# The norm stage by tile, the next half's blocks loaded during the last pair, and a reordered first chunk, in a hybrid conv, HGRN2 and delta-rule layer

## The chip, the cores and the metric

The kernel runs on one core of one Trainium2 chip. The metric is the device time of one execution in microseconds; the median of three runs stands for the kernel. TensorE, VectorE (DVE), ScalarE (ACT), GpSimd (POOL) and SyncE (SP, which only issues DMAs here) run in parallel, each in the order of its own program, and meet at semaphores.

## The reference

One layer on 2048 tokens of 1024 channels. A projection of the normalised input feeds three mixers (a short convolution, HGRN2, a gated delta rule in chunks), whose results are merged by sigmoid gates:

```python
h = rmsnorm(x, norm_w)
proj = einsum('bsd,dc->bsc', h, w_in)        # split into 15 parts
gates = sigmoid(g_all + b_gate)
y_a = (a_b * causal_dwconv(a_c * a_x, conv_a) * silu(a_z)) @ w_out_a
y_b = (head_rmsnorm(hgrn2_chunked(q, k, v, log_f), w) * silu(b_z)) @ w_out_b
y_c = (head_rmsnorm(gated_delta_chunked(q, k, v, log_a, beta), w) * silu(c_z)) @ w_out_c
merged = gates[0] * y_a + gates[1] * y_b + gates[2] * y_c
out = rmsnorm(x + merged @ w_o, final_norm_w)
```

The delta rule solves (I + M) s = rhs for each chunk, M being strictly lower triangular; the kernel's chunks are 128 tokens.

## The kernel before

Five parts run one after the other, each in its own function, with a barrier of all engines between them: `constants`, `norm_and_transpose`, `project`, `recur` and `merge`.

`norm_and_transpose` goes over the 16 tiles t of 128 tokens. ScalarE's `statistics(t)` squares and sums a row of x and makes the reciprocal root; VectorE's `normalise(t)` scales x into `xn`; TensorE's `turn(t)` transposes it in eight 128x128 pieces into PSUM; VectorE's `weigh(t)` multiplies by the norm's weights and writes it. Tiles 0 to 7 (the first half of the tokens) stay on the chip in `hraw`, as four blocks B11, B12, B21, B22 of 512 channels by 512 tokens; tiles 8 to 15 go to DRAM (`h_scratch`) through `ht`, a ring of four tiles. Beside it TensorE forms 16 small columns (beta and the decay) with `sums_of(g)`, once for each group of four tiles, `columns_of(g)` turns them, and `table(g)` copies them. The projection multiplies in Strassen's way with seven products P1 to P7: for each, a combination of the blocks is split into a high part (`h_high`, fp32r, by ScalarE) and a low part (`h_low`, the rest). GpSimd makes the lows of P1, P2 and P5, VectorE those of P3, P7, P6 and P4 and the four block sums (`block_sum`). Dictionaries `after` put these steps behind certain tiles. SP loads x into `xin` (three tiles), and after the last store the first weights.

`project` goes over 80 pairs of column tiles, 40 on each half of the tokens. Pair p has seven products of 12 matmuls (128x512): TensorE's order is P1(p), P4(p-1), P2(p), P3(p-1), P6(p), P5(p), P7(p), and both of pair 39's late ones follow at once. ScalarE copies X to m1, u2 and u3 between products and splits the next weights (`high_part`), GpSimd makes their lows (`low_part`), VectorE their sums and takes the results into `craw`. SP loads weights of pair p+2 and stores results from a `ring` of four slots. After pair 39 the blocks of the second half are needed: `load_tokens` waits for its last product and loads four 1 MB blocks into `h_low`, `token_sums` (DVE) makes the four combinations in `craw`, `ring` and `work`, `token_highs` (ACT) and `token_lows` (POOL and DVE) split them, each in one piece in the engines' programs.

`recur` goes over 16 chunks w. For each the inverse of I + M is built: the 16x16 blocks on the diagonal by substitution on VectorE (`blocks_out` takes ak through DRAM into `X`, `substitute`, `inverses_back` through DRAM into `TT` and `R`), then three levels of doubling on TensorE (`level_w`, `level_z`), then r, e, o and the state. Work of chunk w+1 and the scores of HGRN2 are interleaved. Ahead of chunk 0 come the columns, its key norms, decays (`log_decays`, `betas`, `weighted_decays` on GpSimd), products and its inverse's blocks; `fill_masks` on GpSimd makes the masks. `T`, `R` and `b_g` in the trace are TT, R and the PSUM banks G.

## Time and profile before

| what | value |
|---|---|
| median of 3 runs (2977.01 to 2982.47) | 2977.89 us |
| profiled execution, its own time | 2978.44 us |
| its span, from the first instruction to the last | 2976.7 us |
| TensorE busy in matmuls, share of the span | 2761.7 us, 93% |
| VectorE, ScalarE, GpSimd busy | 1868.9, 1236.1, 1545.4 us |
| mean granted TensorE clock, share of full speed | 0.968 |

A timeline row reads: start and length in us, engine, line of the kernel, operation, out<-in by the program's names (buffer numbers left out), shapes, count of instructions merged, and in brackets how long the engine was idle before it and what ended that. Where rows are merged, the length is that of the whole stretch. Ends of matmuls are modelled, so that consecutive ones seem to overlap; their starts are exact. PEclk is the clock granted to TensorE as a share of 2.4 GHz, so 0.50 is 1.2 GHz.

### The profile page before, as it was taken

How to read it: one execution, taken by the hardware profiler on the slowest of the kernel's cores; microseconds unless marked ns; L12 is line 12 of the kernel's file. 1: busy time of each engine (PE TensorE's matmuls, PEld its weight loads, DVE VectorE, ACT ScalarE, POOL GpSimd, SP SyncE). 2: the span in 40 equal slices, each digit the busy share in tenths (PEclk: the TensorE clock that was granted, in tenths of full speed). 3: DMA queues.
4: the chain of work that ended last, by engine and by line, in shares of the span. 5: the costliest groups of instructions: out<-in, count | busy, mean ns of one | idle time of the engine just before them, and what ended most of it. 6: DMA issues, size and time to landing. Idle time of an engine off the chain costs nothing. (4 is left out here: it accounts for less than half of the span.)

```text
span 2976.7 us, 39010 instructions
## 1 busy us (share of the span) xinstructions
PE 2761.7 (93%) x13943; PEld 2293.6 (77%) x13943; DVE 1868.9 (63%) x2886; ACT 1236.1 (42%) x2144; POOL 1545.4 (52%) x1161
## 2 busy tenths in 40 slices
PE   5799999999987999999999779999999869999999
PEld 2488888888865888888888568888888757787877
DVE  6568778772228778877723278888888643444453
ACT  5244434444443434444444345555555433122221
POOL 1355555455437455555554466676666375353531
PEclk7899999999998999999999989999999989999999
DMA  4332333334441433333333455445555266555552
GB/s 137 97 111 83 119 92 107 107 99 114 113 151 47 120 92 107 104 102 116 92 107 105 123 140 126 126 124 145 147 148 133 54 192 207 153 168 164 165 172 82
DMA packets 535879, 363.92 MB, mean 122 GB/s; under 512 B 65430, under 2 KB 469000, under 8 KB 535688
## 3 DMA queue, kind: packets, MB, share of 16 engines
q1 hardware_dynamic: 535688, 361.43, 42.6%
q8 instruction: 113, 1.85, 0.3%
q14 instruction: 78, 0.64, 0.1%
HBM read 249.17 MB, written 112.20 MB: 121 GB/s over the span
## 5 line engine op out<-in xcount | busy, mean ns | idle before, releaser
L715 POOL TENSOR_TENSOR w_low<-w_raw,w_high 128x512 fp32r<-128x512 f32 x480 | 682.9, 1428 | 623.2 <-ACT w_high L793 623.1
L747 PE MATMUL p_x<-h_high,w_high 128*128 128x512 f32 x1280 | 501.8, 392 | 33.0 <-POOL h_low L722 17.8
L747 PE MATMUL p_x<-h_high,w_low 128*128 128x512 f32 x1280 | 500.4, 391 | 0.0
L747 PE MATMUL p_x<-h_low,w_high 128*128 128x512 f32 x1280 | 500.4, 391 | 0.0
L793 ACT ACTIVATE w_high<-w_raw 128x512 fp32r<-128x512 f32 x480 | 297.2, 626 | 256.3 <-PE p_z L747 142.5
L747 PEld LDWEIGHTS p_x<-h_high,w_high 128*128 128x128 f32 x1280 | 241.9, 189 | 86.0 <-issue 18.2
L2185 POOL TENSOR_TENSOR m_wo_low<-m_wo_raw,m_wo_high 128x512 fp32r<-128x512 f32 x128 | 172.5, 1352 | 252.7 <-ACT m_wo_high L2275 252.7
L747 PEld LDWEIGHTS p_x<-h_low,w_high 128*128 128x128 f32 x1280 | 241.8, 189 | 50.6
L747 PEld LDWEIGHTS p_x<-h_high,w_low 128*128 128x128 f32 x1280 | 242.0, 189 | 50.0
L2226 PE MATMUL b_o<-m_yh,m_wo_high 128*128 128x512 f32 x512 | 208.1, 406 | 55.5 <-POOL m_wo_low L2185 31.9
L747 PE MATMUL p_z<-h_high,w_high 128*128 128x512 f32 x640 | 249.0, 389 | 0.0
L747 PE MATMUL p_z<-h_high,w_low 128*128 128x512 f32 x640 | 249.0, 389 | 0.0
L747 PE MATMUL p_z<-h_low,w_high 128*128 128x512 f32 x640 | 249.0, 389 | 0.0
L1009 DVE TENSOR_TENSOR c_raw<-p_z,u 128x512 f32<-128x512 f32 x72 | 49.8, 691 | 250.8 <-PE p_x L747 181.3
L2226 PE MATMUL b_o<-m_yh,m_wo_low 128*128 128x512 f32 x512 | 206.1, 403 | 0.0
L2226 PE MATMUL b_o<-m_yl,m_wo_high 128*128 128x512 f32 x512 | 205.5, 401 | 0.0
L2275 ACT ACTIVATE m_wo_high<-m_wo_raw 128x512 fp32r<-128x512 f32 x128 | 80.7, 631 | 282.8 <-PE b_o L2226 234.3
L2319 DVE TENSOR_TENSOR m_tmp<-b_o,m_gt 128x512 f32<-128x512 f32 x96 | 66.4, 692 | 205.2 <-PE b_o L2226 144.9
L715 POOL TENSOR_TENSOR w_low<-w_s,w_high 128x512 fp32r<-128x512 f32 x80 | 115.0, 1438 | 96.1 <-ACT w_high L793 95.5
L2226 PEld LDWEIGHTS b_o<-m_yh,m_wo_high 128*128 128x128 f32 x512 | 100.3, 196 | 82.0 <-POOL m_wo_low L2185 35.5
L1369 POOL TENSOR_TENSOR dx<-hin 128x256 f32<-128x256 f32 x112 | 76.9, 686 | 158.7 <-ACT hx L1720 157.1
L1025 DVE SCALAR_TENSOR_TENSOR ring<-c_raw,cols,ring 128x512 f32<-128x512 f32 x128 | 142.5, 1113 | 4.6
(282 smaller groups left out, 6131.8 us busy)
## 6 DMA issues: line engine op xcount, KB each, us to landing
w_raw<-in_w_in_dram SPq DMA_DIRECT2D x160, 512.0 KB, 5.2
branch_scratch<-ring SPq DMA_DIRECT2D x176, 256.0 KB, 5.2
gate_scratch<-ring SPq DMA_DIRECT2D x96, 256.0 KB, 6.0
m_gt<-gate_scratch SPq DMA_DIRECT2D x96, 256.0 KB, 3.8
hin<-branch_scratch SPq DMA_DIRECT2D x16, 1280.0 KB, 11.0
zin<-branch_scratch SPq DMA_DIRECT2D x16, 1024.0 KB, 6.4
m_yl<-y_scratch SPq DMA_DIRECT2D x16, 1024.0 KB, 10.3
m_wo_raw<-in_w_out_c_dram SPq DMA_DIRECT2D x64, 256.0 KB, 2.9
```

The costliest lines, as they stand in the source:

```text
L715: nc.gpsimd.tensor_tensor(wl[:, j, :, :], place(p, j), wh[:, j, :, :].bitcast(F32), ALU.subtract).then_inc(low, 1)
L747: x = nc.tensor.matmul(to[:], w[:, j, k, :], h[:, j, k, :], start=(opens and k == 0 and a == 0), stop=(k == HK - 1 and a == 2), skip_group ...
L793: fn(wh[:, j, :, :], place(p, j), ACT.Copy).then_inc(high, 1)
L1009: tt(of_unit(p, 1, 1), Z[p % 2][:], u3[:], ALU.add).then_inc(c22, 1)
L1025: link(stt(out, src, w, out, ALU.mult, ALU.add))
L1369: tt(free_ap(dx[:, l % 2, :], 0, halves), left, mid, ALU.subtract)
L2185: tt(wl[:, u % SLOTS, :, :], wraw[:, u % SLOTS, :, :], raw(wh[:, u % SLOTS, :, :]), ALU.subtract).then_inc(w_low, 1)
L2226: x = nc.tensor.matmul(bank, w[:, u % SLOTS, k, :], y[:, 4 * i + k, :], start=(i < 3 and k == 0 and a == 0), stop=(i != 2 and k == 3 and a ...
L2275: fn(wh[:, u % SLOTS, :, :], wraw[:, u % SLOTS, :, :], ACT.Copy).then_inc(w_high, 1)
L2319: tt(to, bank, gt[:, b, :], ALU.mult).then_inc(gated, 1)
```

## The change

**Norm stage.** The sums are made tile by tile (`sums_of(t)`, eight products of 128 columns instead of eight of 512 for each group). All seven low parts and the block sums are VectorE's; GpSimd has no work in the stage. `normalise(t)` is ScalarE's from tile 8 on. `xin` has four tiles, `xn` three, `ht` two; SP loads the first weights ahead of the last five stores.

TensorE at the start of the stage, before (with seven more rows of this kind to its end):

```order
L356 MATMUL ps_h<-ident,xn 128x128 x40
L367 MATMUL ps_s<-hraw,wsm 16x512 x8
L356 MATMUL ps_h<-ident,xn 128x128 x24
L375 MATMUL ps_s<-ident,small 128x16 x4
L356 MATMUL ps_h<-ident,xn 128x128 x8
```

and after it:

```order
L366 MATMUL ps_h<-ident,xn 128x128 x16
L378 MATMUL ps_s<-hraw,wsm 16x128 x8
L366 MATMUL ps_h<-ident,xn 128x128 x8
L378 MATMUL ps_s<-hraw,wsm 16x128 x8
L366 MATMUL ps_h<-ident,xn 128x128 x8
```

The transposes of tile t+1 stand between the sums of two tiles; at the end of the stage the sums of one tile are left in place of those of four.

**Change of halves.** `load_tokens`, `token_sums`, `token_highs` and `token_lows` are gone. Each block goes by `load_block` to a place that is free early: b11 to `work`, b12 to the low part of P2, b22 to that of P6, b21 to that of P5, and b21 and b22 once more, to those of P4 and P3. P7's sum is made in two halves in a new tile `t3`, so the places free up earlier. SP issues these loads between its stores within pair 39, ScalarE and VectorE have their steps between those of pairs 39 and 40; GpSimd makes P3's low only.

VectorE around the change of halves, before; `c_raw<-p_z,u` are the takes of pair 39, `w_s<-w_raw` begins the weight sums of pair 41:

```order
L1009 TENSOR_TENSOR c_raw<-p_z,u 128x512
L1014 TENSOR_TENSOR c_raw<-p_z,u 128x512
L956 TENSOR_TENSOR c_raw<-h_low 128x2048
L959 TENSOR_TENSOR c_raw<-h_low,c_raw 128x2048
L962 TENSOR_TENSOR ring<-h_low,c_raw 128x2048
L963 TENSOR_TENSOR work<-h_low 128x2048
L967 TENSOR_TENSOR h_low<-c_raw,h_high 128x2048
L967 TENSOR_TENSOR h_low<-work,h_high 128x2048
L967 TENSOR_TENSOR h_low<-ring,h_high 128x2048
L971 MEMSET c_raw 128x4x3
L979 TENSOR_TENSOR w_s<-w_raw 128x512
```

and after it, from the last sum that is made within pair 39:

```order
L1010 TENSOR_TENSOR work<-h_low,work 128x2048
L1077 TENSOR_TENSOR c_raw<-p_z,u 128x512
L1016 TENSOR_TENSOR t<-h_low 128x1024
L1023 TENSOR_TENSOR c_raw<-h_low,work 128x2x1024
L1041 TENSOR_TENSOR h_low<-t,h_high 128x1024
L1016 TENSOR_TENSOR t<-h_low 128x1024
L1082 TENSOR_TENSOR c_raw<-p_z,u 128x512
L1041 TENSOR_TENSOR h_low<-h_low,h_high 128x2048
L1041 TENSOR_TENSOR h_low<-c_raw,h_high 128x2048
L1041 TENSOR_TENSOR h_low<-work,h_high 128x2048
L1030 TENSOR_TENSOR ring<-h_low,c_raw 128x2048
L1041 TENSOR_TENSOR h_low<-t,h_high 128x1024
```

P5's sum (L1010) now stands ahead of the take of c22, and P1's low three rows before it; P7's pieces are on both sides of the take of c12.

SP in the same place has, in place of one group of four loads behind all stores, these rows within pair 39 (load, stores, loads by turns):

```order
L693 DMA work<-h_scratch 128x4x512
L712 DMA gate_scratch<-ring 128x512 x3
L693 DMA h_low<-h_scratch 128x4x512 x2
L712 DMA gate_scratch<-ring 128x512
L693 DMA h_low<-h_scratch 128x4x512
L683 DMA w_raw<-in_w_in_dram 128x8x128 x2
L712 DMA gate_scratch<-ring 128x512 x2
```

Before, the weights stood ahead of all of pair 38's stores, and the blocks behind all of pair 39's.

**First chunk.** The squares of chunk 0 are ScalarE's and its `betas` VectorE's; GpSimd goes from `log_decays(0)` to the masks and `weighted_decays(0)`, and `pairs` and the squares of chunk 1 come behind. VectorE splits the log decays before it clears the states. The mask `later` is gone (it is ones minus `causal`). Chunk 0's diagonal blocks are inverted in the bank G[1] instead of M[0], which frees M[0] for other products in that time, and these are moved ahead of its inverse: v, k, hv, products_ks, scores 0 to 2 of chunk 0 and the decays and products of chunk 1.

TensorE in front of chunk 0's first inverse product (`b_g<-T,ak`), before:

```order
L1473 MATMUL b_m<-qkn 128x256 x4
L1446 MATMUL b_m<-sq,ones 128x512 x2
L1484 MATMUL b_m<-ident,zin 128x128 x8
L1494 MATMUL b_m<-S,qkn 128x256 x4
L1543 MATMUL b_g<-T,ak 128x128 x8
L1500 MATMUL b_m<-ident,qkn 128x128 x4
```

and after it (`b_h<-kql` are the scores; behind it level_z follows at once):

```order
L1577 MATMUL b_m<-S,qkn 128x256 x4
L1583 MATMUL b_m<-ident,qkn 128x128 x4
L1589 MATMUL b_m<-ident,hin 128x128 x4
L1609 MATMUL b_h<-kql 128x128 x4
L1533 MATMUL b_m<-la_t,later_r 128x512 x4
L1609 MATMUL b_h<-kql 128x128 x4
L1533 MATMUL b_m<-la_t,ones_r 128x512 x4
L1556 MATMUL b_m<-qkn 128x256 x4
L1609 MATMUL b_h<-kql 128x128 x4
L1626 MATMUL b_g<-T,ak 128x128 x8
```

Eight groups of matmuls that stood behind the first inverse product now stand ahead of it. The core of the diff:

```diff
@@ norm_and_transpose @@
-    XIN, XN, SETS = 3, 2, 3
+    XIN, XN, HT, SETS = 4, 3, 2, 3
...
-                for t in range(1, T):
+                for t in range(2, T):
                     load(t)
-                    if t - 3 >= first:
-                        store(t - 3)
-                for t in range(T - 3, T):
-                    store(t)
+                    if t - XIN - 1 >= first:
+                        store(t - XIN - 1)
                 for u, col in enumerate(front["first"]):
                     sp.dma_start(front["raw0"][:, u, :, :], io["w_in"][0, :, col:col + P].rearrange("(k p) c -> p k c", p=P)).then_inc(w0_in, 16)
-                for i in range(per):
-                    sp.wait_ge(h_out[i], 16 * ((T - first) // per))
+                for t in range(T - XIN - 1, T):
+                    store(t)
...
+                    if t >= first:
+                        normalise(t)
...
-                after = {8: [lambda: block_sum(P5)], 9: [lambda: block_sum(P7), lambda: table(0), lambda: low(P3)], 10: [lambda: block_sum(P6)],
-                         11: [lambda: low(P7)], 12: [lambda: block_sum(P4), lambda: table(1)], 13: [lambda: low(P6)], 14: [lambda: low(P4)], 15: [lambda: table(2)]}
+                after = {5: [lambda: low(P1)], 6: [lambda: low(P2)], 7: [lambda: table(0)], 8: [lambda: block_sum(P5)],
+                         9: [lambda: block_sum(P7), lambda: low(P3)], 10: [lambda: block_sum(P6)], 11: [lambda: block_sum(P4), lambda: low(P5)],
+                         12: [lambda: table(1), lambda: low(P7)], 13: [lambda: low(P6)], 14: [lambda: low(P4)], 15: [lambda: table(2)]}
...
-                def sums_of(g):
-                    pe.wait_ge(weighed, 2 * per * (g + 1))
-                    if g >= 2:
+                def sums_of(t):
+                    g, u = t // per, t % per
+                    pe.wait_ge(weighed, 2 * t + 2)
+                    if g >= 2 and u == 0:
                         pe.wait_ge(tabbed, g - 1)
                     for k in range(K):
-                        h = hraw[:, 2 * (k // HK) + g, k % HK, :] if g < 2 else ht[:, :, k, :]
-                        x = nc.tensor.matmul(ps_s[g % 2][0:2 * V, :], wsm[:, k, :], h, start=(k == 0), stop=(k == K - 1))
+                        h = hraw[:, 2 * (k // HK) + g, k % HK, u * P:(u + 1) * P] if t < first else ht[:, t % HT, k, :]
+                        x = nc.tensor.matmul(ps_s[g % 2][0:2 * V, u * P:(u + 1) * P], wsm[:, k, :], h, start=(k == 0), stop=(k == K - 1))
...
@@ project @@
+        b_place = {"b11": work[:], "b12": lows_of(P2), "b22": lows_of(P6), "b21": lows_of(P5), "b21_again": lows_of(P4),
+                   "b22_again": lows_of(P3)}
+        b_free = {"b12": P2, "b22": P6, "b21": P5, "b21_again": P4, "b22_again": P3}
+        b_block = {"b11": (0, 0), "b12": (0, 1), "b22": (1, 1), "b21": (1, 0), "b21_again": (1, 0), "b22_again": (1, 1)}
...
+        b_order = (P1, P5, (P7, 0), P6, P2, (P7, 1), P4, P3)
+        sum_order = (P5, (P7, 0), P6, (P7, 1), P4)
+        pool_lows, dve_lows = (P3,), (P1, (P7, 0), P2, P6, P5, (P7, 1), P4)
...
+                    if p in last_of and p + 1 < N:
+                        sb, late = pairs[p][0] + 1, [x for x in results if x[0] == p]
+                        load_block(sb, "b11")
+                        for x in own[:-1]:
+                            store(x)
+                        load_block(sb, "b12")
+                        load_block(sb, "b22")
+                        store(own[-1])
+                        load_block(sb, "b21")
+                        load_weights(p + 2)
+                        for x in late[:2]:
+                            store(x)
+                        load_block(sb, "b21_again")
+                        store(late[2])
+                        load_block(sb, "b22_again")
+                        store(late[3])
+                        continue
...
+                    half_ends, sb = p in last_of and more, pairs[p][0] + 1
+                    if half_ends:
+                        token_low(sb, P1)
                     if q is not None:
                         finish_mid(q)
                         take_c12(q)
                     if more:
                         fourth_sum(p + 1)
+                    if half_ends:
+                        token_sum(sb, P5)
...
+                            token_sum(sb, (P7, 0))
+                            token_sum(sb, P6)
+                            token_low(sb, (P7, 0))
+                            token_sum(sb, (P7, 1))
                         take_c12(p)
                         finish_late(p)
                         finish_last(p)
-                        if more:
-                            token_sums(pairs[p][0] + 1)
+                        if half_ends:
+                            token_low(sb, P2)
+                            token_low(sb, P6)
+                            token_low(sb, P5)
+                            token_sum(sb, P4)
+                            token_low(sb, (P7, 1))
...
+                    if p in last_of and more:
+                        token_high(pairs[p][0] + 1, P1)
+                    if p - 1 in last_of:
+                        token_high(pairs[p][0], P4)
...
+                        token_high(pairs[p][0], P3)
                     if q is not None:
                         finish_late(q)
                     if more:
                         high_part(p + 1, P5)
+                    if p in last_of and more:
+                        token_high(pairs[p][0] + 1, P5)
...
+                            token_high(pairs[p][0] + 1, (P7, 0))
                         if p in x_by_act:
                             from_x(p)
                         finish_mid(p)
+                        if more:
+                            token_high(pairs[p][0] + 1, P6)
+                            token_high(pairs[p][0] + 1, P2)
+                            token_high(pairs[p][0] + 1, (P7, 1))
...
@@ recur @@
-        XP = free_ap(M[0][0:V * NB, 0, :], 0, [[SUB, SUB], [1, SUB]])
+        XP = lambda v: free_ap((M[0] if v > 0 else G[1])[0:V * NB, 0, :], 0, [[SUB, SUB], [1, SUB]])
...
-                squares(0)
-                pool.wait_ge(split, 3)
+                pool.wait_ge(split, 2)
                 log_decays(0)
-                betas(0)
                 fill_masks(pool, more_masks, masks_set, masks_cut)
+                weighted_decays(0)
+                differences(0, 0)
+                squares(1)
                 tt(pairs[:], keep["ident"][:], more_masks["upper"][:, 0, :], ALU.add).then_inc(pairs_set, 1)
-                weighted_decays(0)
-                squares(1)
+                differences(0, 1)
                 log_decays(1)
                 betas(1)
-                differences(0, 0)
                 pool.wait_ge(cols, 2)
...
+                turn_v(0)
+                norms(1)
+                pe.wait_ge(zeroed, 4)
                 pe.wait_ge(col_exp, 1)
-                norms(1)
+                products_ks(0)
+                turn_k(0)
+                turn_hv(0)
+                scores(0, 0)
+                decays_between(1)
+                scores(0, 1)
+                decays_from_start(1)
+                products_kq(1)
+                scores(0, 2)
...
+                copy_v(0)
+                level_exp(0, 0)
                 blocks_in(0)
+                key_norms(1)
+                copy_k(0)
+                copy_hv(0)
+                level_exp(0, 1)
+                from_start_h(0)
                 inverses_out(0)
-                key_norms(1)
-                level_exp(0, 0)
+                decays_between(1)
+                decays_from_start(1)
+                level_exp(0, 2)
...
+                pair_kq(0)
                 unit_diagonal(0)
                 substitute(0, range(SUB - 2, 0, -1))
+                dve.wait_ge(cols, 2)
+                residual(0)
+                keys(1)
                 dve.wait_ge(masks_cut, 2 * LEVELS + 2)
                 dve.wait_ge(pairs_set, 1)
-                dve.wait_ge(cols, 2)
+                level_kq(0, 1)
+                pair_scores(0)
+                an_keys(1)
+                an_queries(1)
...
```

## Rows read from the trace of the kernel before

**Rows 1.** Windows: us, busy and count of PE, PEld, DVE, ACT, POOL, PEclk, DMA share, GB/s

```profile
24.00:28.00 4.00, 3.62 (x11) 1.85 (x11) 1.57 (x3) 2.39 (x2) 0.40 (x1) 0.50 0.72 252
28.00:32.00 4.00, 4.00 (x10) 0.93 (x9) 2.85 (x1) 3.90 (x8) 4.00 (x1) 0.92 0.01 4
...
1150.00:1200.00 50.00, 50.00 (x223) 41.40 (x222) 46.34 (x47) 20.86 (x35) 26.91 (x19) 1.00 0.31 88
```

**Rows 2.** Timeline of TensorE, norm stage to the first product

```profile
24.43 1.97 PE L356 MATMUL ps_h<-ident,xn 128*128 128x128 f32 x8 [0.38 <-DVE xn L395]
...
34.45 1.10 PE L356 MATMUL ps_h<-ident,xn 128*128 128x128 f32 x8
...
71.26 9.60 PE L367 MATMUL ps_s<-ht,wsm 128*16 128x512 f32 x16 [1.43 <-DVE ht L407]
...
114.18 0.79 PE L747 MATMUL p_x<-h_high,w_high 128*128 128x512 f32 x1 [7.50 <-POOL w_low L715]
```

**Rows 3.** Timeline of TensorE, change of halves

```profile
878.65 0.39 PE L747 MATMUL p_z<-h_low,w_high 128*128 128x512 f32 x1
896.83 0.76 PE L747 MATMUL p_x<-h_high,w_high 128*128 128x512 f32 x1 [17.79 <-POOL h_low L722]
...
912.12 0.77 PE L747 MATMUL p_y<-h_high,w_high 128*128 128x512 f32 x1 [9.83 <-POOL h_low L722]
...
930.88 0.50 PE L747 MATMUL p_x<-h_high,w_high 128*128 128x512 f32 x1 [3.02 <-ACT u L922]
...
948.09 0.79 PE L747 MATMUL p_x<-h_high,w_high 128*128 128x512 f32 x1 [3.30 <-ACT u L912]
```

**Rows 4.** Timeline of TensorE, first chunk of the recurrence

```profile
1734.83 2.05 PE L1543 MATMUL b_g<-T,ak 128*128 128x128 f32 x16 [0.48 <-DMA T<-inverse_scratch]
...
1755.01 1.95 PE L1566 MATMUL b_g<-r,R 128*128 128x128 f32 x16
```

**Rows 5.** Timeline of VectorE, norm stage

```profile
29.15 3.53 DVE L395 TENSOR_SCALAR xn<-xin,stat 128x1024 f32<-128x1024 f32 x1 [3.58 <-ACT stat L317]
...
41.54 1.29 DVE L407 TENSOR_TENSOR hraw<-ps_h,cols 128x512 f32<-128x512 f32 x2 [0.17 <-PE ps_h L356]
...
51.91 2.29 DVE L428 TENSOR_TENSOR hraw<-hraw 128x2048 f32<-128x2048 f32 x1 [4.42 <-PE ps_s L367]
```

**Rows 6.** Timeline of ScalarE, norm stage

```profile
12.98 1.06 ACT L313 ACTIVATE xn<-xin 128x1024 f32<-128x1024 f32 x1 [2.42 <-DMA xin<-in_x_dram]
...
14.82 1.06 ACT L313 ACTIVATE xn<-xin 128x1024 f32<-128x1024 f32 x1
...
105.62 0.59 ACT L330 ACTIVATE small<-ps_s 16x512 f32<-16x512 f32 x1 [16.46 <-PE ps_s L367]
```

**Rows 7.** Timeline of ScalarE, change of halves

```profile
872.66 0.60 ACT L922 ACTIVATE u<-p_x 128x512 f32<-128x512 f32 x1 [2.09 <-PE p_x L747]
...
886.71 1.91 ACT L802 ACTIVATE h_high<-h_low 128x2048 fp32r<-128x2048 f32 x1 [4.88 <-DMA h_low<-h_scratch]
```

**Rows 8.** DMA issues in 8 to 112: count, KB each, median us to landing

```profile
h_scratch<-ht SPq DMA_DIRECT2D x8, 512.0 KB, 3.4
```

**Rows 9.** Timeline of SP, change of halves

```profile
880.92 2.48 SPq L666 DMA_DIRECT2D h_low<-h_scratch  x4
```

**Rows 10.** Timeline of VectorE, change of halves

```profile
898.88 6.53 DVE L962 TENSOR_TENSOR ring<-h_low,c_raw 128x2048 f32<-128x2048 f32 x1
```

**Rows 11.** Timeline of GpSimd, first chunk of the recurrence

```profile
1694.72 3.80 POOL L1348 TENSOR_TENSOR la_t<-causal,la_parts 128x1024 fp32r<-128x1024 f32 x2
...
1700.79 0.84 POOL L124 MEMSET upper<- 128x896 f32 x1
...
1709.82 2.34 POOL L1358 TENSOR_TENSOR dec<-dec,db 128x1024 f32<-128x1024 f32 x1
```

**Rows 12.** Timeline of VectorE, first chunk of the recurrence

```profile
1690.88 0.29 DVE L1999 TENSOR_TENSOR la_parts<-ab,la_parts 128x128 fp32r<-128x128 f32 x1
...
1726.70 0.17 DVE L1891 TENSOR_TENSOR b_m<-b_m,part 64x14 f32<-64x14 f32 x1
```

332 lines of the change are left out of this document (187 added, 145 removed).

## The prediction

> **What bounds the kernel now.** I went first by the timeline of TensorE, looking for stretches in which it does not start its next matmul at once. In a settled stretch of the projection it starts one every 50 / 223 = 0.224 us [rows 1], and nothing here is faster than that. Three places differ, and the change touches these three: the normalisation stage in front of the first product at 114.18 [rows 2], the change of halves after the matmul at 878.65 [rows 3], and the first chunk of the recurrence, whose first inverse product starts at 1734.83 [rows 4]. So I cost each place by itself, as the time at which TensorE gets back to its regular work, and add the three. The projection between them and the merge behind them are left as they are; what is gained in front of a place moves it as a whole. The profiled execution took 2978.44 us (span 2976.7); the sum is made against that and 0.5 us taken off for the median 2977.89.
>
> **Part 1, the normalisation.** What is there now: a group of sums is one burst of 9.60 us on TensorE [rows 2], and VectorE waits for it (4.42 us ahead of the block sum at 51.91) [rows 5]; a normalisation that meets GpSimd's low parts takes 3.53 us [rows 5] where the shape costs about 0.75. VectorE finishes the weighing of tile 7 at 41.54 + 1.29 = 42.8 [rows 5]; the small copy of the last group starts at 105.62 [rows 6], and from there to the first product are 114.18 - 105.62 = 8.6 us of short steps that the change keeps.
>
> The first eight tiles after it: ScalarE's statistics take 14.82 - 12.98 = 1.84 us a tile [rows 6], but high(P1) still waits for tile 3, and VectorE now carries low(P1) and low(P2), 2 x 2.29 [rows 5], where GpSimd's collisions used to cost about as much. TensorE adds a quarter of a group (9.60 / 4 = 2.4) to 1.10 or 1.97 of transposes per tile [rows 2]. I walk this to 44.6, 1.8 later than now.
>
> The last eight: VectorE has 8 weighings of 1.29, 4 block sums and 5 lows of 2.29 [rows 5]: 10.3 + 20.6 = 30.9 us. ScalarE, which takes over the eight normalisations (about 1.06 each, as its square of the same 128x1024) [rows 6], has 8 x (1.84 + 1.06) + 5 x 1.91 [rows 6, 7] + 2 x 0.59 = 33.9, of which the first tile lies ahead of 44.6: 31.0. Two engines that hand work to each other with nearly equal sums do not run without waits, and a weighing also waits for the store two tiles before (3.4 us to land [rows 8], behind a load, and from tile 13 on behind the first weights too). I add 4: the weighing of tile 15 ends at 44.6 + 30.9 + 4 = 79.5. Then one tile's sums (2.4), the copy and the 8.6 to the first product: 90.5, and 2.5 more for matmuls at the lower clock: 93. **Gain 114.2 - 93 = 21.** Ends: no waits and full clock give 27; the rival below gives 10.
>
> TensorE's order is now eight transposes of a tile, then eight products of 128 columns for the sums of the tile before; it works in short bursts. In the trace it was granted 0.50 (1.2 GHz) in 24 to 28, after transposes with waits between them, and 0.92 in 28 to 32, once sums kept it busy without a gap [rows 1]. The Trainium skill (TensorE: Matmul & The Clock Gate, section A second HAM failure mode: psum-queue depth-cycling) says that small idles between groups of matmuls make the clock go down and up, and that the stream loses by it. The trace agrees in part, by the fall to 0.50; by that rule the first product would be later by the 9 to 12 us of rival 1.
>
> **Part 2, the change of halves.** Now: the last matmul starts at 878.65; the next are at 896.83, 912.12, 930.88 and, after 60 more, 948.09 [rows 3]. Between 878.65 and 948.09 stand 132 matmuls (11 products of 12), 29.6 us at 0.224: 69.4 - 29.6 = **39.8 us are lost**. The load is issued at 880.92 [rows 9], the first 1 MB is used at 886.71 [rows 7], 5.8 us later, and sums and lows follow one another, one of them stretched to 6.53 by GpSimd [rows 10] against 2.29 alone [rows 5].
>
> After: the first block goes to `work` some 26 us earlier, the others as the last products of the low parts that they overwrite end (a product is 12 x 0.224 = 2.7 us, pair 39 has its seven up to 878.9). P1's high and low are made inside the pair, so product P1 of pair 40 starts right behind P3 of pair 39. What it costs there: ScalarE's u3 copy (872.66 now, [rows 7]) stands behind high(P5), which waits for b12, issued after the stores of pair 38 that it follows in SP's queue. b12 lands about 868.8, sum and high add 2.3 (more beside GpSimd) and 1.9: u3 at 874.4 instead of 872.7. **-1.7.** The rest is VectorE's chain from u3 on: take_c22, half of P7's sum (1.2), P6's sum (2.3), low of the half, the other half's sum, then low P2, low P6, low P5 (2.2 each), sum P4, low of the other half (the rows stand with the change). Walked from u3, the lows end so: P2 done at 885.1, P6 887.3, P5 889.5, P7 892.8, P4 897. TensorE: P1 880.5, P2 waits until 885.2 (2.0 lost), P6, P5 without wait, P7 waits for u2, which ScalarE copies only after high(P4), which needs sum P4 at 891.7: 895.9 (2.5 lost). P3 is cut by GpSimd after 898.3 and needed at 906.8: covered, with 2 us to spare if it takes 6.5. At the place of 948.09 the wait hangs on VectorE's convolution of pair 40, which starts when weights 42 land; they are issued about 30 us earlier, the wait stays, 2.7. Sum: 1.7 + 2.0 + 2.5 + 2.7 = 8.9 lost in place of 39.8. **Gain 30.5** (I round down for the seams). Ends: 34 with no collision on the ports, 20 with rival 2.
>
> The stores of pair 39 and the weights 41 move behind block loads on SP's queue; they are late by 3 to 6 us, and their readers (ring slots, early_sums(41) at 893) come later still. Nothing.
>
> **Part 3, the first chunk.** GpSimd's weighting of dec starts at 1709.82 [rows 11], after squares, la_t (3.80), db, the masks (from 1700.79) and pairs. Now it is la_t (after la_parts, which VectorE makes first: 1689.5 instead of 1691.2 [rows 12]), masks with 1709.82 - 1700.79 = 9.0, then dec: 1689.5 + 3.8 + 9.0 = 1702.3, **7.5 earlier**. The masks stay in front of it; dec itself is ready at about 1700. From there the chain through DRAM (store, X, substitution until 1726.70 [rows 12], store, T) is as long as before, so T is there at 1734.83 - 7.5 = 1727.3.
>
> But TensorE now has scores(0,2) ahead of its first inverse product, and that needs level_kq(0,2), which stands on VectorE behind residual, keys(1), an_keys(1) and an_queries(1), all behind the substitution (ends 1719.4). Walked: 11 us at full clock, 15 at half. So the inverse product starts between 1730.5 and 1734.5; I take 1732.5. In return it is not interleaved: before, 20.2 us pass from there to the product with r at 1755.01 [rows 4]; 20 matmuls of 128 columns at 0.11 (1.10 for eight, in [rows 2] a little over it), 8 of 512 at 0.224 and 4 of 256 at twice a column's cost leave: 2.2 + 1.8 + 1.8 = 5.8. 20.2 - 5.8 = 14.4, so r's product starts at 1746.9: **gain 8**. Behind it nothing moved. Ends: 13.3 (7.5 + 5.8, no gate) and 2.
>
> **Sum.** 21 + 30.5 + 8 = 59.5; 2978.4 - 59.5 - 0.5 = 2918.4, **2918**.
>
> **Rivals.**
> 1. TensorE stays at 1.2 GHz through the second eight tiles: 1.97 + about 3.5 (a quarter group without the faster half) = 5.5 a tile, 44 us instead of 34.9, and the tail 2 longer: gain 10, time **2929**. For it: 0.50 in [rows 1]. Against: at that pace it would have no gaps, and the same rows show the clock rising when it has none. 0.13.
> 2. Port collisions at the change of halves: five 2048-wide operations of VectorE behind u3, each longer by 2 (the row shows up to 4.2 more [rows 10]). Gain 20, **2929**. Against: GpSimd has no weights to cut between 877 and 887. 0.13.
> 3. The gate in the first chunk eats all of its gain: **2926**. 0.08.
> 4. Slower: the two-deep `ht`. Each tile's weighing waits for a store that SP issues behind a load whose slot waits for ScalarE. If load, store and weighing ran one after the other (4 + 3.4 + 1.3 = 8.7 a tile, 70 us for eight), part 1 would lose 14 instead of gaining 21: 2953. It turns the whole slower only from 59.5 + 35 more, at 8.7 + 3.5 = about 13 us a tile: **2990**. Against it: 3.4 to land is for 512 KB alone, and the loads are four tiles ahead. 0.02.
> 5. The planned order does not start earlier at one of the three places, because a wait that I took as met is not: 2940. 0.03.
>
> **Chances.** Forecast 0.61 (2908 to 2927 by itself). Cases 1 to 3 lie at 2926 to 2929 and two together near 2937; the upper ends of all three gains together give 2904. Range **2903 to 2936**. A measurement of this kernel tells about 0.2%, 6 us, from no change. Faster 0.97, same 0.01, slower 0.02.
>
> **What would show it.** First product of the projection near 93, with sums of 2 to 3.5 us behind every tile's transposes; if it is above 100, look at the granted clock there. At the change of halves no gap over 4 us, product P1 of pair 40 within 3 us of the last one of pair 39, a gap ended by ScalarE's u ahead of P7. T's product near 1732 less what is gained before it (about 51), so near 1681, ended by VectorE's kql and not by the DMA of T; 14 to 15 us from it to r's product. Wrong is the forecast if GpSimd or a DMA ends a wait of over 5 us in one of them.

## The result, and the profile after

| | before | after |
|---|---|---|
| median | 2978.34 us (2977.01 to 2982.47, 4 runs) | 2924.90 us (2924.39 to 2925.99, 4 runs) |
| ratio | | 0.9819, 95% interval 0.9802 to 0.9836 |
| profiled execution, span | 2978.44, 2976.7 us | 2925.99, 2924.3 us |
| mean granted clock | 0.968 | 0.979 |

The kernel is 53.4 us faster; 2918 was forecast, and 59.5 us of gain. I read the three places again as I had read them before: the time at which TensorE gets back to its regular work.

**The normalisation.** Timeline of TensorE (start, us, instruction, then in brackets the idle time ahead of it and what ended it), from the last tile's sums to the first product of the projection:

```profile
77.09 1.92 PE L378 MATMUL ps_s<-ht,wsm 128*16 128x128 f32 x16
79.69 0.42 PE L386 MATMUL ps_s<-ident,small 16*128 16x16 f32 x4 [0.68 <-ACT small L338]
87.61 0.80 PE L788 MATMUL p_x<-h_high,w_high 128*128 128x512 f32 x1 [7.50 <-POOL w_low L758]
```

The first product starts at 87.61 instead of 114.18 [rows 2]: 26.6 gained. The windows of this stage (length, then busy time and count of PE, PEld, DVE, ACT and POOL, the granted clock, DMA share, GB/s) hold the main surprise, the clock:

```profile
24.00:28.00 4.00, 4.00 (x35) 3.15 (x34) 2.51 (x4) 0.53 (x1) 0.00 (x0) 1.00 0.59 221
28.00:32.00 4.00, 3.01 (x26) 2.39 (x27) 0.98 (x2) 3.94 (x6) 0.00 (x0) 1.00 0.02 6
...
48.00:52.00 4.00, 3.18 (x15) 2.47 (x16) 1.58 (x3) 3.90 (x7) 0.00 (x0) 0.60 0.53 118
52.00:56.00 4.00, 4.00 (x35) 3.27 (x33) 4.00 (x3) 3.90 (x7) 0.00 (x0) 0.97 1.09 349
...
72.00:76.00 4.00, 3.68 (x33) 2.99 (x31) 4.00 (x5) 1.55 (x3) 0.00 (x0) 1.00 0.62 177
```

Of the 4 us windows between 24 and 80 only the two shown at 48 and 52 are below 1.00; before, 24 to 28 had 0.50 [rows 1], and so had all five windows from 56 to 76. Ahead of 24 the windows say 1.00 too, but there the first sixteen transposes took 3.65 us (from 15.57 on), the pace of the low clock: eight of them take 1.97 us at 0.50 and 1.09 at 1.00. VectorE was to set the pace of the last eight tiles, and it does: it waits for only 3.1 of 33 us. These are its groups in 44.1 to 77.1 (busy us, mean ns, then idle time and its releaser):

```profile
L443 DVE TENSOR_TENSOR h_low<-hraw,h_high 128x2048 fp32r<-128x2048 f32 x5 | 11.4, 2279 | 0.0
L418 DVE TENSOR_TENSOR ht<-ps_h,cols 128x512 f32<-128x512 f32 x16 | 10.2, 680 | 2.4 <-PE ps_h L366 2.4
L437 DVE TENSOR_TENSOR hraw<-hraw 128x2048 f32<-128x2048 f32 x4 | 9.1, 2284 | 0.7 <-DVE ht L418 0.7
```

**The change of halves.** Timeline of TensorE; it starts a matmul every 0.227 us between the rows, so what stands in brackets is what is lost by waiting:

```profile
846.28 0.39 PE L788 MATMUL p_x<-h_low,w_high 128*128 128x512 f32 x1
851.95 0.79 PE L788 MATMUL p_x<-h_high,w_high 128*128 128x512 f32 x1 [5.27 <-ACT u L972]
...
864.53 0.47 PE L788 MATMUL p_y<-h_high,w_high 128*128 128x512 f32 x1 [1.38 <-DVE h_low L1041]
...
876.18 0.50 PE L788 MATMUL p_x<-h_high,w_high 128*128 128x512 f32 x1 [3.15 <-ACT u L958]
...
903.29 0.79 PE L788 MATMUL p_x<-h_high,w_high 128*128 128x512 f32 x1 [7.73 <-ACT u L958]
```

In order: P4 of pair 39, then P2 and P7 of pair 40, then P7 of pair 41. From the last matmul ahead of the first of these waits (846.28 here, 872.23 in the kernel before) to P7 of pair 41 (903.29, and 948.09 [rows 3]) it is 57.0 us after and 75.9 before. I call this stretch the change of halves from here on; all numbers for it below are between the same two matmuls. 156 matmuls stand in it, 35.4 us at one every 0.227. So it gained 18.9, or 18.2 if counted from the first product (948.09 - 903.29 - 26.6), against 30.5 forecast.

**The first chunk.** Timeline of TensorE:

```profile
1685.17 1.16 PE L1609 MATMUL b_h<-kql 128*128 128x128 f32 x8 [2.57 <-DVE kql L2034]
1686.16 1.95 PE L1626 MATMUL b_g<-T,ak 128*128 128x128 f32 x16
...
1700.79 1.95 PE L1649 MATMUL b_g<-r,R 128*128 128x128 f32 x16
```

From the last product of the projection (1638.52; 1683.29 before) to the product with r it is 62.3 us; before it was 1755.01 [rows 4] - 1683.29 = 71.7. Gain 9.4. The three places give 26.6 + 18.2 + 9.4 = 54.2, and the span is shorter by 52.4: 1.8 is given back behind the first chunk, where nothing was changed.

### The profile page after: what moved, and what is told of

Same layout as the page of the kernel before. It is cut to its first block and busy times, and to the rows that moved or that the text cites. A ratio compares the mean times of both kernels' runs of the same rounds, so it can differ in the third digit from the quotient of the medians.

```text
span 2924.3 us, 39400 instructions
## 1 busy us (share of the span) xinstructions
PE 2757.2 (94%) x14135; PEld 2308.6 (79%) x14135; DVE 1853.6 (63%) x2886; ACT 1244.2 (43%) x2154; POOL 1506.4 (52%) x1151
## 6 DMA issues: line engine op xcount, KB each, us to landing
m_yl<-y_scratch SPq DMA_DIRECT2D x16, 1024.0 KB, 10.6
```

## Experiments: the three parts apart

Each of the first three kernels takes whole functions from one of the two kernels. The two lines of each cut here name the functions and stand for all of their lines.

**The normalisation of before in the changed kernel.**

```diff
-norm_and_transpose as changed
+norm_and_transpose as before
```

> The changed kernel with the normalisation of the kernel before; change of halves and first chunk stay changed. Theory A (the three places add up, and each is worth what the starts in the changed kernel's trace say: 26.6, 18.2 and about 9.4): the first product of the projection is back near 114.2, the time is 2924.9 + 26.6 = 2951.5. Theory B (the sizes of the prediction, 21, 30.5 and 8, are the right ones, and the trace of one execution misleads): 2924.9 + 21 = 2946. Theory C (the earlier start of the projection was partly lost again later, by the 1.8 us that the end of the kernel gives back, or by the slow clock at the first products): 2950 or less.

Measured: 2952.79 us (2949.90 to 2955.34), ratio 0.9913 (0.9898 to 0.9928), first product at 114.25. The part is worth 2952.8 - 2924.9 = 27.9: theory A. Within the spread of these runs (5.4 us) nothing of the earlier start was lost later.

**The projection of before in the changed kernel.**

```diff
-project as changed
+project as before
```

> The changed kernel with the projection of the kernel before, so with its old change of halves. Theory A (by the starts): the idle times of 17.8, 9.8, 3.0 and 3.3 us come back, 26.6 earlier than in the kernel before, and the time is 2924.9 + 18.2 = 2943.1. Theory B (the prediction's term): 2924.9 + 30.5 = 2955.4.

Measured: 2939.81 us (2937.29 to 2946.48), ratio 0.9873 (0.9858 to 0.9889). In the medians the part is worth 14.9; the stretch is 76.1 us in its trace, 19.1 more than in the changed kernel. Both rule out 30.5. The two numbers differ by 4, and how much a profiled execution can differ is seen behind the projection: from its last product to the end of the span the profiled kernels whose recurrence and merge are word for word the same took 1284.9 (norm_as_before), 1285.8 (changed), 1288.2 (b12_first), 1290.0 (three_mended) and 1283.6 (conv_before_sums). The profiled execution of halves_as_before took 1289.7 there, 3.9 more than that of the changed kernel, which is nearly all of the 4. So I size an edit below by its stretch, and use the medians for what the kernel is worth. The stretch itself repeats well: in four kernels with the same projection it is 57.0 (changed), 56.8 (norm_as_before), 56.9 (sums_by_group) and 56.7 (scores_behind_inverse). A single wait in it does not: the last one is 7.73, 6.10, 6.10 and 7.74 in these four, and where it is shorter the matmuls ahead of it took longer. So a change of the last wait by 1.6 us shows nothing, and one of the stretch by under 0.4 neither.

**The recurrence of after in the kernel before.**

```diff
-recur, hybrid_trunk as before
+recur, hybrid_trunk as changed
```

> The kernel before with the recurrence of the changed kernel alone. Theory A (by the starts): the product with r starts 9.4 us earlier, and the end gives up to 1.8 of it back: 2978.3 - 9.4 = 2969, up to 2971. Theory B (the prediction's term): 2978.3 - 8 = 2970. Theory C (the first chunk gains only because the projection's last stores and the first loads now meet elsewhere): no change, 2978. The first inverse product still starts behind VectorE's kql in A and B.

Measured: 2970.45 us (2967.45 to 2974.09, 9 runs), ratio 0.9975 (0.9964 to 0.9985): 8.4 gained, A or B, not C. From the last product of the projection to the product with r it is 1744.43 - 1680.78 = 63.7. Together the three give 27.9 + 14.9 + 8.4 = 51.2 of 53.4: within the spread of the medians the parts add up.

## Experiment: what gained in the normalisation

```diff
-XIN, XN, HT, SETS = 4, 3, 2, 3
+XIN, XN, HT, SETS = 4, 3, 4, 3
...
-                        h = hraw[:, 2 * (k // HK) + g, k % HK, u * P:(u + 1) * P] if t < first else ht[:, t % HT, k, :]
+                        h = hraw[:, 2 * (k // HK) + g, k % HK, :] if t < first else ht[:, :, k, :]
...
-                    if t > 0:
+                    if t > 0 and t % per == 0:
                         sums_of(t - 1)
```

> The changed kernel with the small sums done four tiles at once again (8 products of 512 columns in one go) and a four-deep ht; the normalisations of the last eight tiles stay on ScalarE, the lows on VectorE. Theory A (the short bursts of sums in each tile are what kept TensorE's granted clock at 1.00, and their delay to VectorE is small): the clock falls to 0.50 again in some stretches between 20 and 80, a group of sums costs up to 9.6 us in one piece and weighings wait for it; the first product is 5 to 10 us later, time 2930 to 2935. Theory B (the gain of the stage comes from the work of the last eight tiles being shared out, the sums' order is worth nothing): first product within 2 us of 87.6, time 2924 to 2927. Theory C (prediction's rival 1, bursts cost clock): the first product is earlier than 87.6, time 2920.

Measured: 2941.24 us (2940.65 to 2944.34), ratio 0.9877 (0.9862 to 0.9891); first product at 102.85, 15.2 later than in the changed kernel and more than even theory A said. Its TensorE rows for two of the four groups, and the windows there:

```profile
41.36 9.22 PE L378 MATMUL ps_s<-hraw,wsm 128*16 128x512 f32 x16 [3.71 <-DVE hraw L418]
...
84.32 9.93 PE L378 MATMUL ps_s<-ht,wsm 128*16 128x512 f32 x16 [6.90 <-DVE ht L418]
```

```profile
60.00:64.00 4.00, 1.92 (x11) 1.68 (x11) 4.00 (x4) 3.90 (x6) 0.00 (x0) 0.50 0.91 263
...
84.00:88.00 4.00, 3.68 (x5) 0.72 (x6) 0.40 (x2) 0.00 (x0) 0.00 (x0) 0.50 0.46 131
88.00:92.00 4.00, 4.00 (x8) 0.75 (x7) 0.00 (x0) 0.00 (x0) 0.00 (x0) 0.73 0.00 0
```

Half of the 15.2 is in the body: VectorE, which waits 8.05 and 5.08 us for groups of sums, ends its last weighing at 84.26 instead of 77.04. The other half is behind it: a whole group (9.93) instead of one tile's sums (1.92) stands between the last weighing and the small copy. The granted clock is 0.50 in five of the windows (40, 56, 60, 80 and 84), around TensorE's waits of 3.71 us (ended at 41.36), 5.75 (58.24) and 6.90 (84.32). So of the 26.6, some 15 go with the order of the sums (and the four-deep `ht` that the groups need). The other 11 belong to the rest of the change in this stage (normalisations on ScalarE, lows on VectorE, the depths of the rings, the order of the loads), which I did not separate.

## Experiments: the waits at the change of halves

**b12 earlier** (the first wait, 5.27).

```diff
                         load_block(sb, "b11")
+                        load_block(sb, "b12")
                         for x in own[:-1]:
                             store(x)
-                        load_block(sb, "b12")
```

> The changed kernel; on SP's queue the load of block b12 is issued ahead of the three stores of pair 38 that it follows now. In the changed kernel's trace P4 of pair 39 waits 5.27 us for ScalarE's u3, which stands behind high(P5), which waits for sum P5, which waits until 847.11 for b12 (issued at 839.96, 7.1 us to land). Theory A (b12's issue behind the stores is the cause): issued near 836, landed near 843, the wait falls to 1 to 2 us, TensorE's clock stays at 1.00 behind it and 2.6 us more come back: 2924.9 - 3.5 to -6.5, so 2918.5 to 2921.5. Theory B (the transfer is slowed by what runs beside it, so b12 lands about 847 anyway): same time, 2925. Theory C (the later waits, on P2, P7 of pair 40 and P7 of pair 41, grow by what this one gives): 2923 to 2925.

Measured: 2924.19 us (2923.74 to 2925.15), ratio 0.982 (0.9804 to 0.9837), no difference that a measurement can tell from the changed kernel. The stretch is 54.9 (changed: 57.0). b12 is issued at 835.27 and its landing no longer holds VectorE; but the timeline of VectorE has, in order:

```profile
842.62 1.76 DVE L1059 TENSOR_TENSOR w_raw<-w_raw 128x512 f32<-128x512 f32 x1 [2.33 <-POOL w_low L758]
844.30 3.37 DVE L1010 TENSOR_TENSOR work<-h_low,work 128x2048 f32<-128x2048 f32 x1
```

In the second row the sum of P5 now stands behind the weights' sum, which waits for GpSimd, and takes 3.37 beside GpSimd instead of 2.29. The wait is still 4.10. So A named a cause, but another stood right behind it: the stretch is 2.1 shorter.

**u3 before high(P5)**, the order of ScalarE alone.

```diff
-                    if p in last_of and more:
-                        token_high(pairs[p][0] + 1, P5)
                     act.wait_ge(prod, product_no[p, P7])
...
                         high_part(p + 1, P7)
+                    if p in last_of and more:
+                        token_high(pairs[p][0] + 1, P5)
```

> The changed kernel; ScalarE copies u3 of pair 39 (and makes the high part of pair 40's P7) first and high(P5) of the new half behind them, not ahead. Loading b12 earlier had taken only 1.2 us off the wait of 5.27 (to 4.10), because VectorE's sum P5 then stood behind fourth_sum and met GpSimd (3.37 us). Theory A (the order of ScalarE makes the wait: u3 has no need of that sum): the gap at P4 of pair 39 is gone (under 0.8 us), TensorE's clock stays at 1.00 behind it, and from the last product before it to P7 of pair 41 it takes 57.0 - 5.3 - 3 = 49 us: time 2924.9 - 8 = 2917. Theory B (VectorE's chain, which needs sum P5 and then P6, P2 and P5's lows, is as late as before and the waits on P2 of pair 40, P5 and P7 grow by what this one gives): 54 to 57 us, time 2922 to 2925.

Measured: 2919.22 us (2917.99 to 2922.03), ratio 0.9802 (0.9788 to 0.9817), stretch 53.3. Between the theories: the first wait is gone, and a part of it comes back one step later.

```profile
860.24 0.47 PE L788 MATMUL p_y<-h_high,w_high 128*128 128x512 f32 x1 [4.70 <-DVE h_low L1041]
```

P2 of pair 40 waits 4.70 for its low part instead of 1.38: VectorE's chain starts from the landing of b12 (its sum of P5 at 846.84), not from u3, and at P2's low it waits 1.23 more for ScalarE's high. P2 starts at 860.24 against 864.53, 3.9 earlier if both are counted from the start of the stretch (860.24 - 845.93 = 14.3; 864.53 - 846.28 = 18.3).

**high(P4) later** (the third wait, 3.15).

```diff
-                    if p - 1 in last_of:
-                        token_high(pairs[p][0], P4)
...
                     fn(u2[:, p % 2, :], X[p % 2][:], ACT.Copy).then_inc(u2_ready, 1)
+                    if p - 1 in last_of:
+                        token_high(pairs[p][0], P4)
```

> The changed kernel; ScalarE makes high(P4) of the new half behind the copy of u2 of pair 40 instead of ahead of the weights' highs and of u2. Theory A (u2 hangs behind high(P4), which waits for VectorE's sum P4 until 872.18, and GpSimd's weight lows hang behind it too): the wait of 3.15 us ahead of P7 of pair 40 goes, GpSimd's lows come about 4 us earlier, so weights 42 are issued earlier and the wait of 7.73 ahead of P7 of pair 41 shrinks to 3 to 5: 2924.9 - 6 to -8, so 2917 to 2919. Theory B (only the first wait goes; the second hangs on weights 42 alone): 2921 to 2922. Theory C (P4's low comes too late for product P4 of pair 40 and the wait moves there): 2924 to 2926.

Measured: 2925.76 us (2923.53 to 2926.59), ratio 0.9825 (0.981 to 0.984), stretch 57.0, unchanged: theory C, in part. P7 of pair 40 still waits 2.51, now for its own low part and no longer for u2; P4 of pair 40 waits 0.86, and P7 of pair 41 as long as before (7.48).

**The low part of P3 on VectorE** (the last wait, 7.73).

```diff
-        pool_lows, dve_lows = (P3,), (P1, (P7, 0), P2, P6, P5, (P7, 1), P4)
+        pool_lows, dve_lows = (), (P1, (P7, 0), P2, P6, P5, (P7, 1), P4, P3)
...
                     take_c11(p)
+                    if p - 1 in last_of:
+                        token_low(pairs[p][0], P3)
```

> The changed kernel; the low part of P3 of the new half is made by VectorE, behind take_c11 of pair 40, not by GpSimd (where it took 5.06 us at 880.92 and the low parts of pair 41's weights stood behind it until 888.49). Theory A (GpSimd's queue holds early_sums(42), so the convolution of pair 40, so u2 of pair 41): early_sums(42) starts when weights 42 are there, 886.6 instead of 888.6, and the stretched steps behind it (1.69, 1.67, 1.47, 2.44 us where they take 0.69, 0.69, 0.49 and 1.5 alone) are short again; the wait of 7.73 ahead of P7 of pair 41 falls to 2 to 4: 2924.9 - 4 to -6, so 2919 to 2921. Theory B (the DMA of weights 42 is the cause): the wait falls by under 2: 2923 to 2925. Theory C (VectorE's fourth sum and c22 come later by 2.3 us and TensorE waits for them): 2925 to 2927.

Measured: 2922.77 us (2921.53 to 2925.18), ratio 0.9817 (0.9803 to 0.9832), stretch 55.7, last wait 6.72. Nearer to B than to A. early_sums(42) starts at 885.97 instead of 888.59, now ended by the landing of weights 42 (issued at 880.38), and the stretch is 1.0 to 1.3 shorter: GpSimd's 5 us were not the whole of it.

**The three together.**

> The three edits of b12_first, p4_high_late and p3_low_on_vector together. If the causes are those named and their gains add: lost at the change of halves about 1.5 + 1.4 + 0 + 3 in place of 17.5, and the slow clock behind the first wait gone too: 2924.9 - 12 to -15, so 2910 to 2913, which is what the prediction had forecast for this place (a gain of 30.5 in place of 18.2). If they share one cause, the sum is less than that of the three: 2914 to 2919.

Measured: 2921.66 us (2921.01 to 2923.97), ratio 0.9814 (0.9799 to 0.9829). Stretch 53.1: 3.9 less, a little over the 2.1 + 0 + 1.3 of the three alone, and far from the 12 to 15 expected. The waits are 4.21, 1.28, 2.51 and 4.19. Why they stay is seen on VectorE and GpSimd. GpSimd now gets the weights' highs while VectorE makes the tokens' lows, and both are slow:

```profile
862.75 10.41 POOL L758 TENSOR_TENSOR w_low<-w_raw,w_high 128x512 fp32r<-128x512 f32 x4 [12.35 <-ACT w_high L832]
...
863.12 3.38 DVE L1039 TENSOR_TENSOR h_low<-work,h_high 128x2048 fp32r<-128x2048 f32 x1
866.43 3.39 DVE L1028 TENSOR_TENSOR ring<-h_low,c_raw 128x2048 f32<-128x2048 f32 x1
```

Four low parts take 10.41 us, 2.6 each, where one alone takes 1.29, and VectorE's operations take 3.38 and 3.39 where 2.29 is usual. Weights 42 are issued right behind the four (873.18), and that is 7.8 earlier than in the changed kernel, so it is not they that hold the last wait now: from 858.71 on VectorE is never idle until u2 is copied, and its own chain, lengthened beside GpSimd, ends last.

**The first convolution ahead of early_sums(42).**

```diff
+                    if p - 2 in last_of:
+                        finish_early(q)
                     if more:
                         early_sums(p + 1)
-                    if q is not None:
+                    if q is not None and p - 2 not in last_of:
                         finish_early(q)
```

> The changed kernel; in pair 41's turn VectorE does the first convolution of pair 40 ahead of early_sums(42), not behind. In the changed kernel's trace VectorE is idle for 6.48 us before early_sums(42) at 888.59, then the convolution is stretched by GpSimd's low parts, and ScalarE's u2 of pair 41 waits for it: TensorE idles 7.73 us. Theory A (the convolution stands behind a wait for weights 42 and GpSimd that it has no need of): it starts near 882, ScalarE's two silus come 5 to 6 us earlier, the wait falls to 2 to 3: time 2924.9 - 5 = 2919 to 2920. Theory B (the weights' own chain, early_sums(42) to fourth_sum(42) and u2, then ends last): the wait falls by less than 2: 2923 to 2925.

Measured: 2924.36 us (2921.22 to 2924.74), ratio 0.9816 (0.9801 to 0.9831), stretch 56.1, little below the 56.7 to 57.0 of the same projection: nearer to theory B. The first convolution starts at 880.10, but u2 stands behind two, and the second still comes behind the sums of pair 42. Timeline of its ScalarE, the two silus and u2:

```profile
890.70 0.63 ACT L857 ACTIVATE ring<-ring 128x512 f32<-128x512 f32 x1 [0.24 <-DVE ring L1095]
899.37 0.63 ACT L857 ACTIVATE ring<-ring 128x512 f32<-128x512 f32 x1 [8.03 <-DVE ring L1095]
899.90 0.58 ACT L958 ACTIVATE u<-p_x 128x512 f32<-128x512 f32 x1
```

## Experiments: the gate in the first chunk, and all together

```diff
-                scores(0, 2)
                 for w in range(win):
...
+                    if w == 0:
+                        scores(0, 2)
                     level_z(w, 4)
```

> The changed kernel; in the first chunk TensorE does scores(0,2) behind the first inverse products (T with ak) and not ahead of them. In the changed kernel T was issued for its load at 1680.11 and the first inverse product started at 1686.16 behind VectorE's kql. Theory A (the gate costs what the prediction said, 5.2 us less the transfer's own lateness): the inverse product starts near 1683 against the last projection product at 1638.5, 3 us earlier, and all behind it moves: 2924.9 - 3 = 2922. Theory B (the kql is on the way to r in any case, since level 5 and the residual products follow it): the product with r starts within 1 us of 1700.8: 2924 to 2926.

Measured: 2924.57 us (2923.16 to 2925.49), ratio 0.982 (0.9804 to 0.9836). Timeline of its TensorE:

```profile
1681.59 2.05 PE L1626 MATMUL b_g<-T,ak 128*128 128x128 f32 x16 [1.46 <-DMA T<-inverse_scratch]
```

Counted from the last product of the projection (1635.95) that is 45.6, and 47.6 in the changed kernel; to the product with r 61.1 against 62.3. The gate costs 2.0 at the first inverse product and 1.1 at r, too little for the medians: theory B. How far this second distance repeats is seen in the kernels that leave this part alone: it is 62.2 to 62.6 in the five others whose first inverse product takes 1.95 us, and 63.9 to 64.5 in the four (b12_first, p4_high_late, three_mended, sums_by_group) in which it takes 3.18 to 3.54.

**All of them, and both convolutions first.** The edits of three_mended, u3_before_p5_high and scores_behind_inverse, and:

```diff
                     if p - 2 in last_of:
                         finish_early(q)
+                        finish_mid(q)
```

> The changed kernel with the edits of three_mended, u3_before_p5_high and scores_behind_inverse together, and with both convolutions that ScalarE's u2 of pair 41 stands behind put ahead of early_sums(42) (conv_before_sums had moved the first alone, and the wait had only gone from 7.7 to 5.3, since the second still stood behind the sums of pair 42). Measured by the stretch from the last product ahead of P4 of pair 39 to P7 of pair 41: 57.0 us in the changed kernel, 53.1 in three_mended, 53.3 in u3_before_p5_high. Theory A (the causes are apart, so their gains add, and the second convolution was the one that held u2): 57.0 - 3.9 - 3.7 - 3 = 46.4, of which 35.3 is matmuls, and 1.1 more in the first chunk: 2924.9 - 11.7 = 2913. Theory B (they share VectorE's chain of sums and lows, which then ends last whatever stands first): 50 to 52 us, time 2917 to 2920, with the waits on P2 and P7 of pair 40 grown to over 4.

Measured: 2915.99 us (2913.89 to 2918.88, 5 runs), ratio 0.9791 (0.9778 to 0.9804): the best version, 8.9 us below the changed kernel in the medians and between the two theories. Its stretch:

```profile
845.28 0.50 PE L786 MATMUL p_x<-h_high,w_high 128*128 128x512 f32 x1 [0.69 <-ACT u L968]
...
857.55 0.47 PE L786 MATMUL p_y<-h_high,w_high 128*128 128x512 f32 x1 [3.81 <-DVE h_low L1039]
...
890.70 0.50 PE L786 MATMUL p_x<-h_high,w_high 128*128 128x512 f32 x1 [1.64 <-ACT u L954]
```

From 844.21 to 890.70 it is 46.5, and theory A had 46.4. The last wait fell to 1.64, from 4.19 in three_mended; that fits the second convolution as what held it (the rows of conv_before_sums say the same), but no run moved the two convolutions alone. The waits at P2 (3.81) did grow, as B said. Two things take some of the gain away. P4 of pair 41 now waits 2.21 for u3, just behind the stretch. And the first inverse product finds TensorE at the low clock (row, and window of four us):

```profile
1673.93 3.55 PE L1630 MATMUL b_g<-T,ak 128*128 128x128 f32 x16 [2.21 <-DMA T<-inverse_scratch]
```

```profile
1674.00:1678.00 4.00, 4.00 (x21) 4.00 (x22) 0.24 (x1) 1.08 (x2) 4.00 (x3) 0.57 1.19 304
```

3.55 us for what took 1.95 in the changed kernel at 1.00. That this comes from the edits is not shown: four kernels that leave this place alone had it too, as said above. The product with r comes 63.6 behind the projection, 1.3 later than in the changed kernel and not 1.1 earlier.

## Why the prediction was right, and where not

**In the whole** the time (2924.9) lies in the range and near the forecast of 2918; the places, their order of size and the sign are as said. But 59.5 hides an error of +5.6, one of -12.3 and one of +1.4, and 1.8 given back at the end; without the first the forecast would have been off by nearly twice as much. That the whole came out so near is in part luck: errors of opposite sign.

**Normalisation: 21 forecast, 26.6 measured.** Weighing 7 ends at 44.0 (44.6 forecast), weighing 15 at 77.0 (79.5): VectorE's 30.9 of work was right, its waits were 3.1 (the rows above) and not 4, and its operations overlap a little. The term that was most off is the tail: 10.6 from there to the first product instead of 13.5, of which 2.5 were put down to matmuls at the lower clock; the granted clock stayed at 1.00 until the small products were done (80), and a tile's sums took 1.92 and not 2.4. The body gave 1.9 more and the first eight tiles 0.6. Rival 1, the second eight tiles at 1.2 GHz, is ruled out: from 22 us on eight transposes took 1.09 and a tile's sums 1.92, but for those at 48.82 and 50.72 (1.97 and 2.65), behind a wait of 2.80 us. By the rule of the Trainium skill (TensorE: Matmul & The Clock Gate, section A second HAM failure mode: psum-queue depth-cycling) small idles between groups should have cost clock. This case's trace agrees in one place only, behind the idle of 2.80; behind those of 0.29 to 1.64 us between 30 and 77 the clock stayed at 1.00. sums_by_group has fewer and longer idles, and 0.50 in the windows shown. Rival 4, the two-deep `ht`, did not show: from 44 to 77 VectorE never waited for a store (its two waits stand in the groups above). Its sum was also off: from 2953 another 25 us, and not 59.5 + 35, would have made the kernel as slow as before.

**Change of halves: 30.5 forecast, 18.2 measured.** P1 of pair 40 starts right behind the last product of pair 39, as said, and the four waits stand where the prediction put them, behind the releasers that it named. But "no gap over 4 us" did not hold: two sizes were wrong, and a cost was left out.

- u3: forecast 1.7 later than before, where the wait was 0.7, so 2.4; measured 5.27. The step that failed is "b12 lands about 868.8". With 26.6 off, that is 842.2; it was issued at 839.96 and VectorE had it at 847.11. Two runs show that the landing is only the first cause (b12_first: 4.10 left), and that the order of ScalarE is what makes it a wait of TensorE (u3_before_p5_high: 0.69).
- P2 of pair 40: 2.0 forecast, 1.38 measured. P7 of pair 40: 2.5 forecast, 3.15 measured, behind high(P4) as said.
- P7 of pair 41 (last of the four): 2.7 forecast, 7.73 measured. The step that failed is "they are issued about 30 us earlier, the wait stays, 2.7". It hung on the convolutions, as said, but weights 42 were issued only 21.0 earlier (928.58 - 880.98 - 26.6), and I did not walk what stands ahead of the convolutions: GpSimd, held until 874.69 by ScalarE's highs behind high(P4), then with P3's low (5.06) in between, released early_sums(42) at 888.59, 2.0 behind the landing of weights 42 (ScalarE had them at 886.61). The rows of GpSimd in the changed kernel:

```profile
874.69 6.26 POOL L758 TENSOR_TENSOR w_low<-w_raw,w_high 128x512 fp32r<-128x512 f32 x3 [6.96 <-ACT w_high L834]
880.92 5.06 POOL L763 TENSOR_TENSOR h_low<-h_low,h_high 128x2048 fp32r<-128x2048 f32 x1
885.94 1.29 POOL L758 TENSOR_TENSOR w_low<-w_raw,w_high 128x512 fp32r<-128x512 f32 x1
887.20 1.29 POOL L758 TENSOR_TENSOR w_low<-w_s,w_high 128x512 fp32r<-128x512 f32 x1
```

and of VectorE, the first sum of pair 42 and the end of its wait:

```profile
888.59 1.69 DVE L1047 TENSOR_TENSOR w_s<-w_raw 128x512 f32<-128x512 f32 x1 [6.48 <-POOL w_low L758]
```

The loads of weights 42 (SP) and the sum that they release (VectorE), in the kernel before; and the loads in the changed kernel:

```profile
928.58 13.83 SPq L657 DMA_DIRECT2D w_raw<-in_w_in_dram  x4
934.29 0.69 DVE L979 TENSOR_TENSOR w_s<-w_raw 128x512 f32<-128x512 f32 x1 [2.68 <-DMA w_raw<-in_w_in_dram]
```

```profile
880.98 15.85 SPq L683 DMA_DIRECT2D w_raw<-in_w_in_dram  x4
```

Measured from the moment at which TensorE was ready for P7 (944.6 before, 895.4 after), the weights landed 1.5 later than before, GpSimd held the sums 2.0 more, and the chain from these sums to the end of the first convolution took 9.3 instead of 8.4: together the 4.4 by which this wait grew (3.30 to 7.73). p3_low_on_vector took 1.0 to 1.3 off the stretch, the first convolution alone 0.5 to 0.9, and all edits with both convolutions left a wait of 1.64.

- The clock: left out. Behind the first wait TensorE runs at 1.2 GHz, 12 starts 0.43 apart where 0.227 is normal, about 2.4 us (windows of the changed kernel, then of u3_before_p5_high, where the wait is gone):

```profile
852.00:856.00 4.00, 4.00 (x10) 3.13 (x11) 4.00 (x3) 2.69 (x4) 1.28 (x1) 0.50 1.16 323
856.00:860.00 4.00, 4.00 (x15) 3.21 (x14) 3.41 (x3) 2.36 (x3) 0.00 (x0) 0.78 0.46 107
```

```profile
848.00:852.00 4.00, 4.00 (x19) 3.13 (x19) 4.00 (x4) 2.78 (x3) 2.29 (x1) 1.00 1.07 384
852.00:856.00 4.00, 3.54 (x16) 2.61 (x14) 3.97 (x4) 3.83 (x5) 0.00 (x0) 1.00 1.19 303
```

Against the forecast: 2.9 + 5.0 + 0.7 - 0.6 for the waits, 2.4 for the clock, which is 10.4 of 12.3. Of the rest, 0.6 was lost ahead of the stretch (18.9 against 18.2); the remainder I have not traced to a row. Rival 2, collisions on the ports, came true in part (one low of 3.38 and another of 3.36 where 2.28 is usual), and its price of 10 was nearly the size of the miss, but mostly for another reason: at the last wait 3.5 us came from a late start and 0.9 from the length of VectorE's operations, and at the first wait the operation itself took its usual 2.29. With the orders mended the length shows: in three_mended and all_mended it is in VectorE's chain that the waits remain.

**First chunk: 8 forecast, 9.4 measured** (8.4 alone). The inverse product stands 47.6 behind the projection's last product; the forecast was 1732.5 - 1683.3 = 49.2. From it to r's product it is 14.6 (14.4 forecast), and VectorE's kql ended the wait, as said. That these two agree is in part luck: the eight groups that moved ahead took 7.1 us by their starts in the kernel before, and not 5.8 (0.11 for a product of 128 columns was too low; eight transposes alone take 1.10), while the distance fell by 5.6. Rival 3, the gate that eats the gain, is ruled out; the gate costs 2.0 and not 5.2, half because kql came 1.6 earlier and half because T landed 1.6 later (45.6 against 44.0).

**Left open:** the 1.8 us given back behind the first chunk. Since kernels with the same code there differ by up to 6 us in their profiled execution, it needs no cause in the change, but I have none to show either. Open too is why the same first inverse product is made at the full clock in some profiled executions and at the low one in others.

## What to carry to other kernels

When an engine is ahead of a copy that TensorE waits for, walk its queue up to that copy, and ask of each instruction ahead of it whether the copy needs it; here the order of u3 held 3.7 us of the stretch and the late load of b12 2.1, while high(P4) ahead of u2, which looked the same in the trace, held nothing by itself. A wait that falls uncovers the one behind it: single edits took 0 to 3.7 us off the stretch, the order of every queue together 10.5. Small products for which every tile is ready in turn were here better done tile by tile than saved up: 15 us, since TensorE otherwise stood still in between. And before a row of one trace is put down to an edit, look at the same row in the kernels that leave the place alone.
